# Rotary embedding's exchange of rows: products on the matrix engine, or transfers from SBUF to SBUF

## The reference

```
def apply_rope(x, cos, sin):
    xf = x.astype(jnp.float32)
    half = x.shape[-1] // 2
    x1, x2 = xf[..., :half], xf[..., half:]
    return jnp.concatenate([x1 * cos - x2 * sin, x2 * cos + x1 * sin], axis=-1)
...
proj = h @ w_in[l]
q_m, k_m, v_m, q_d, k_d, v_d, gate_m, gate_d = jnp.split(proj, IN_SPLITS, axis=-1)
qm, km = apply_rope(q_m), apply_rope(k_m)      # 8 heads of 64
qd, kd = apply_rope(q_d), apply_rope(k_d)      # 16 half-heads of 64
```

## Time and profile before

| | us |
|---|---|
| median of 3 runs | 1110.25 |
| lowest and highest | 1108.62, 1110.39 |
| profiled execution, from its first to its last instruction (span) | 1101.0 |

### The profile page before, as it was taken

How to read it: one execution, slowest core, us unless ns; L and a number is a source line. 1 busy time by engine, 2 the same in 40 slices (tenths; PEclk the granted TensorE clock), 3 DMA queues, 4 the chain that set the end, 5 groups by cost and what they waited for, 6 DMA issues and landing times.

```text
span 1101.0 us, 19063 instructions
## 1 busy us (share of the span) xinstructions
PE 917.8 (83%) x8322; PEld 709.9 (64%) x8322; DVE 540.7 (49%) x1004; ACT 347.3 (32%) x678; POOL 61.8 (6%) x81
## 2 busy tenths in 40 slices
PE   5998999999999998999999998666667565667665
PEld 5786787479999887988899975333434333334332
DVE  4446677857888856887866743121211111211121
ACT  3421155236767634545553341010100000000001
POOL 3102710000000000000010000000000000000000
PEclk9899999989999999999999999888878888988889
DMA  9442474474553565654449689999999999999994
GB/s 332 132 161 106 150 276 154 154 229 154 189 194 114 222 223 213 214 202 160 147 159 359 269 323 425 427 424 428 428 429 424 428 427 427 425 429 427 427 428 198
DMA packets 79034, 314.68 MB, mean 286 GB/s; under 512 B 3471, under 2 KB 27312, under 8 KB 62432
## 3 DMA queue, kind: packets, MB, share of 16 engines
q1 hardware_dynamic: 75204, 302.30, 69.7%
q0 software_dynamic: 3600, 11.04, 3.3%
q10 hardware_dynamic: 140, 0.04, 0.0%
HBM read 312.31 MB, written 1.06 MB: 285 GB/s over the span
## 4 chain that ended last, share of the span: by engine, by line
PE 61%; DMA 27%; DVE 6%; ACT 3%; issue 2%; SPq 0%; ACTq 0%; DVEq 0%
PE ps L468 59%; DMA w<-in_w_up 21%; DMA w<-in_w_gate 3%; DMA w<-in_w_down 2%; DMA w<-in_w_in 1%; DVE sp L1794 1%; PE ps L2593 0%; PE ps L553 0%; PE ps L2044 0%; ACT sp L1785 0%; ACT hts L2688 0%; ACT pr L1065 0%; PE ps L978 0%; ACT ht L1833 0%; DVE gm L2239 0%
## 5 line engine op out<-in xcount | busy, mean ns | idle before, releaser
L468 PE MATMUL ps<-w,xg 128*32 128x256 f32 x2048 | 156.4, 473 | 110.8 <-DMA w<-in_w_up 87.4
L468 PE MATMUL ps<-hb,sp 128*128 128x256 f32 x1824 | 229.8, 286 | 0.0
L468 PEld LDWEIGHTS ps<-hb,sp 128*128 128x128 f32 x1824 | 221.4, 190 | 6.9 <-issue 6.2
L468 PEld LDWEIGHTS ps<-w,xg 128*32 128x32 f32 x2048 | 88.2, 135 | 178.2 <-issue 157.2
L1794 DVE TENSOR_TENSOR sp<-w,sp 128x1024 fp32r<-128x1024 f32 x122 | 144.7, 1219 | 42.7 <-ACT sp L1785 42.6
L1785 ACT ACTIVATE sp<-w 128x1024 fp32r<-128x1024 f32 x122 | 122.1, 1050 | 47.7 <-PE ps L468 47.7
L2752 DVE TENSOR_TENSOR cst<-ps,cst 64x256 f32<-64x256 f32 x32 | 13.7, 428 | 227.9 <-ACT cst L2684 227.9
L2684 ACT ACTIVATE cst<-ps 64x256 f32<-64x256 f32 x32 | 12.1, 377 | 328.6 <-PE ps L468 328.6
L2767 DVE TENSOR_TENSOR ost<-ps,cst 32x256 f32<-32x256 f32 x120 | 50.4, 420 | 100.1 <-PE ps L468 97.3
L468 PE MATMUL ps<-w,hts 128*32 128x256 f32 x1024 | 62.1, 382 | 14.8 <-ACT hts L2688 11.1
L468 PE MATMUL ps<-ht,w 128*128 128x256 f32 x256 | 61.6, 400 | 2.3 <-DMA w<-in_w_in 2.2
(11 more groups left out here) (399 smaller groups left out, 1141.4 us busy)
## 6 DMA issues: line engine op xcount, KB each, us to landing
w<-in_w_down SPq DMA_DIRECT2D x36, 2048.0 KB, 36.3
w<-in_w_gate SPq DMA_DIRECT2D x32, 2048.0 KB, 28.3
w<-in_w_up SPq DMA_DIRECT2D x32, 2048.0 KB, 32.3
w<-in_w_in SPq DMA_DIRECT2D x14, 2048.0 KB, 8.8
w<-in_w_up SPq DMA_DIRECT2D x22, 1024.0 KB, 7.6
w<-in_w_ada SPq DMA_DIRECT2D x8, 2048.0 KB, 9.4
w<-in_w_out SPq DMA_DIRECT2D x4, 2048.0 KB, 8.6
w<-in_w_ada POOLq DMA_DIRECT2D x8, 768.0 KB, 4.9
```

The costliest lines, as they stand in the source:

```text
L468: return q.eng.matmul(o, l, r, start=start, stop=stop, skip_group_check=True)
```

## The change

The constant matrix `perm` goes. Its signs move into the table of sines, whose first 32 rows of each head are now negative. Instead of the product, ACT issues four transfers from SBUF to SBUF right after it has evicted a half: each copies 32 partitions of 512 numbers (64 KB) to the place of their partner, in one of two tiles, `rot0` and `rot1` in turn. Before them ACT waits for its own eviction, and from the third rotation on for the rotation two before, which read the same tile. DVE waits for the four transfers and multiplies the tile with the sines in place; the other two instructions stay.

DVE's rotation of half h moves from piece 4(h+1)+2 to piece 4(h+2)+1. The units of the first attention move from pieces 28, 31, 34, 37, 40, 43, 46, 49 to 30, 32, 35, 38, 41, 43, 46, 49; those of the second stay (52, 54, 57, 59, 62, 64, 67, 69). PSUM bank 5 is unused in this stage. A semaphore in the second pass over the experts is replaced by another.

```
@@ const_layout, const_table
-    names = [("ident", 128), ("ones", 128), ("perm", 128), ("cos", 256), ("sin", 256),
+    names = [("ident", 128), ("ones", 128), ("cos", 256), ("sin", 256),
...
-    put("perm", pm)
...
-    put("sin", np.sin(ang).astype(np.float32).T[p % 32])
+    put("sin", np.sin(ang).astype(np.float32).T[p % 32] * np.where(p % 64 < 32, -1.0, 1.0)[:, None])
@@ block_kernel
-        rt = sb("rt", 42144, 512)
+        rot = [sb("rot0", 42144, 512), sb("rot1", 49312, 512)]
...
-        A_AT = [28 + 3 * u if u < 8 else 52 + 5 * (u - 8) // 2 for u in range(NU)]
+        A_AT = [30 + 11 * u // 4 if u < 8 else 52 + 5 * (u - 8) // 2 for u in range(NU)]
...
+        def rotate_sc(q, h):
+            r, src = ROPES.index(h), q_half(h)
+            q.wait_ge(s["q_ev"], h + 1)
+            if r > 1:
+                q.wait_ge(s["rope"], 3 * r - 3)
+            for o, i in ((0, 32), (32, 0), (64, 96), (96, 64)):
+                q.eng.dma_start(rot[r % 2][o:o + 32, :], src[i:i + 32, :]).then_inc(s[f"rot{r % 2}"], 16)
@@ proj2_pe
-                if part == 1 and h - 1 in ROPES:
-                    r = ROPES.index(h - 1)
-                    q.wait_ge(s["q_ev"], h)
-                    mm(q, take(q, 5), C["perm"], q_half(h - 1)).then_inc(s["rope_mm"], 1)
-                    free[5] = [(s["rope"], 3 * r + 1)]
@@ proj2_sc, behind the eviction
+                    if h in ROPES:
+                        rotate_sc(q, h)
@@ proj2_ve
-                if g % 4 == 2 and g // 4 - 1 in ROPES:
-                    h = g // 4 - 1
+                if g % 4 == 1 and g // 4 - 2 in ROPES:
+                    h = g // 4 - 2
                     r = ROPES.index(h)
-                    qv = v(q_half(h), 2)
-                    q.wait_ge(s["rope_mm"], r + 1)
-                    q.wait_ge(s["rope"], 3 * r)
-                    e.tensor_tensor(rtv, v(psum[5], 2), sinb, MUL).then_inc(s["rope"], 1)
+                    qv, rtv = v(q_half(h), 2), rotv[r % 2]
+                    q.wait_ge(s[f"rot{r % 2}"], 64 * (r // 2 + 1))
+                    e.tensor_tensor(rtv, rtv, sinb, MUL).then_inc(s["rope"], 1)
                     e.tensor_tensor(qv, qv, cosb, MUL).then_inc(s["rope"], 1)
                     q.wait_ge(s["rope"], 3 * r + 2)
                     e.tensor_tensor(qv, qv, rtv, ADD).then_inc(s["rope"], 1)
@@ moe_ve, second pass
-                e.tensor_scalar(rk, rk, -float(NSLOT), None, ADD).then_inc(s["m_rk"], 1)
-                q.wait_ge(s["m_rk"], 1)
+                e.tensor_scalar(rk, rk, -float(NSLOT), None, ADD).then_inc(s["m_y"], 1)
+                q.wait_ge(s["m_y"], 5)
```

More of the change, by code:

```diff
@@ L105 @@
         "r_ya", "r_yv", "r_n", "wo_mm", "x1",
-        "hi", "split", "half_mm", "u_z", "u_ev", "u_c", "u_v", "u_s", "a_hi", "a_lo", "dn_mm", "x_ffn", "q_ev", "rope_mm", "rope",
+        "hi", "split", "half_mm", "u_z", "u_ev", "u_c", "u_v", "u_s", "a_hi", "a_lo", "dn_mm", "x_ffn", "q_ev", "rot0", "rot1", "rope",
         "od_sq", "mg_mm", "mg_v", "mg_hi", "mg_lo", "od_mm", "od_n", "od_hi", "od_lo", "o2_mm", "x_mix",
@@ L110 @@
         *["m_" + n for n in ("P", "g_mm", "xg_v", "xg_a", "pw_v", "pw_t", "pw", "gu", "sg", "hh", "tr", "ht",
-                                                "dn", "os", "cb", "y")], "m_rk", "f_a", "f_v"]
+                                                "dn", "os", "cb", "y")], "f_a", "f_v"]
 class Count:
@@ L1970, in block_kernel @@
         Qv = [v(t, 4) for t in Q]
-        rtv = v(rt, 2)
+        rotv = [v(r, 2) for r in rot]
         UNITS2 = [(f, pr, blk) for f in ("moba", "diff") for pr in range(4) for blk in range(2)]
         NU = len(UNITS2)
-        A_AT = [28 + 3 * u if u < 8 else 52 + 5 * (u - 8) // 2 for u in range(NU)]
+        A_AT = [30 + 11 * u // 4 if u < 8 else 52 + 5 * (u - 8) // 2 for u in range(NU)]
         ROPES = (2, 3, 4, 5, 6, 7, 8, 9)
```

## The result

| | us |
|---|---|
| before, median of 7 runs | 1110.12 (1108.13 to 1110.51) |
| changed, median of 7 runs | 1113.58 (1110.33 to 1118.05) |
| ratio | 1.0048, 95% interval 1.0031 to 1.0065 |
| profiled execution of the changed kernel: its time, its span | 1112.72, 1110.9 |

The change makes the kernel slower by 0.48%, 5.3 us by the ratio (3.4 to 7.2 by its interval; the two medians lie 3.5 us apart). The forecast was 1110.8 and no change; the measured time lies 0.08 us above the stated range. A few executions of either kernel ran in a slower state with a lower granted clock, and the ratios leave them out.

The account below looks back on a forecast made before the run. PE was taken to bound the projection stage, DVE close behind. Products saved 3.64 us against 4.2 us of PE waits: +0.55 on span 1101.0, and 9.25 to the median gave 1110.8 us, range 1107.6 to 1113.5 (8 in 10).

Parts of the forecast that it names:

- What bounds the stage: Second block's projections with attention: PE sets the stage, busy 63.21 of 63.38 us; shifts there pass whole to the end.
- The heart: Piece 45: unit 4's probability copy comes behind unit 5's exponentials and the weight copies; PE waits about 3 us.
- DVE and ACT as the chain: From piece 30 on, DVE and ACT hand work to each other in fixed order, so PE alone no longer sets the stage.
- the worked schedule: DVE's and ACT's order followed from half 5's eviction (469.82 us) to unit 5's transposes at 518.1 us.
- The size of a transfer's time: SBUF to SBUF transfers of a half, 4 x 64 KB: landing taken as under 5 us.
- The price of an issue: ACT after each of eight evictions: four DMA issues at 0.36 us each; eviction to next instruction 2.1 us.
- rival B: ACT's issues cost 0.59 us each, holding three evictions on the hand-over 0.9 us longer: +2.7, 1113.5 us; chance 0.14.
- The clock: PE's granted clock behind the wait at piece 45: the sum had no term for a slower clock.
- The saving: Eight permutation products taken off PE in the projection stage, 0.455 us each: 3.64 us.
- The wait for a transfer: DVE's rotations in the projection stage: never wait for the transfers, costed at nothing.
- A: PE stays the projection stage's bound, so 3.64 us come through: 1106.6 us; chance 0.22 with partial gains over 2.2 us.
- C: Transfers land 8 us after issue behind weight loads, delaying half 5's rotation on DVE: +2.4, 1113.2 us; chance 0.06.

Follow-up runs that it names:

- e6: The kernel before with only unit 4 of the first attention moved from piece 40 to 41; ratio 1.0051, stage 144.72 us.
- e2: The changed kernel with all transfers issued by GpSimd's queue between its own loads, none by ACT; ratio 1.0018, stage 143.54 us.
- e16: The changed kernel, its own unit places, with ACT's transfer issues behind the two weight copies of the same piece; ratio 0.9986, stage 140.18 us.
- e4: The changed kernel with the first attention's units three pieces apart from 31, the second's two pieces later; ratio 0.9995, stage 140.15 us.
- e11: The changed kernel with units three pieces apart (31 to 52, second attention from 54) and ACT's issues behind the weight copies; ratio 0.9964, stage 135.30 us.
- e1: The kernel before with only the first attention's units at the changed kernel's places, products kept; ratio 1.0060, stage 146.25 us.
- e3: The changed kernel with two of each half's four transfers issued by ACT and two by GpSimd; ratio 1.0012, stage 142.83 us.
- e5: The changed kernel with unit 4 of the first attention back at piece 40; ratio 1.0024, stage 141.16 us.
- e7: The changed kernel with transfers issued by GpSimd and units three pieces apart (from 31, second attention from 54); ratio 0.9975, stage 137.57 us.

## Why the prediction was wrong

Right, and shown by the traces:
- What bounds the stage, and that what happens in it goes to the end whole: the stage's +5.3 us is the ratio's +5.3.
- The heart: unit 4's copy falls behind unit 5's exponentials and the weight copies, PE waits about 3 us. Measured 3.2 in both profiles of the changed kernel, and made by that one place alone in e6.
- DVE and ACT as the chain. Shifted by the 2.8 us with which the changed profile starts, the worked schedule has the rotation of half 5 end at 482.2, measured 482.6; the maximum of unit 0 at 485.4, measured 485.8. From there each eviction with issues adds what the issues were priced too low, and little else is off.
- The size of a transfer's time: 5.0 us to landing in the median, the edge of the "under 5" that was taken, and up to 7.2. The 3 us that the prediction drew from the Trainium skill (page "DMA: Bandwidth & Descriptors", section "Queues, rings and completion order", the engines' turns between queues) was too short.

Wrong:
- **The price of an issue**, the step "I take 0.36 each". 0.61 was measured, and the hold from eviction to the next ACT instruction is 3.1 us, not 2.1. By unit 2's exponentials the schedule is 2.2 us late, at unit 3's issues 3.2, and so it stays: the probability copy of unit 4 ends at 522.20 (521.83 + 0.37), worked out 516.2 + 2.8 = 519.0. This is rival B in its place and its size: it had 0.59 an issue and three of them on the hand-over, +2.7. That its 1113.5 meets the median of 1113.58 is luck beyond that: against the kernel before it said +3.3, the ratio and the stage say +5.3, and the 2 us in between are the clock (below, 1.4) and 0.5 us more lateness than it had. I gave it 0.14 on the ground that only one issue at the start was that long; those were issues of a few rows or a small block from HBM, not of 32 rows of SBUF, and the row did not bear on it. The figure of the Trainium skill that the prediction set beside it (page "DMA: Bandwidth & Descriptors", section "Anatomy of one DMA", about 50 ns of dispatch) is further off as a price for the engine: the row of the profile, which holds the whole issue and not the dispatch alone, is 0.61 us on ACT, and 0.50 on GpSimd, the path for which it is told.
- **The clock**, a term that the sum did not have. A wait of 3.2 us is followed by 1.2 GHz: unit 5's transposes come 77.11 us after the first row of projection products with PE's full rate (448.42), and 71.93 before (445.62); of these 5.2 us 0.55 were forecast, 3.2 are the copy's lateness against the schedule, and about 1.4 are the clock. The prediction put nothing for it and gave no reason; the one wait of this kind in the trace before, of 1.44 us, had no such tail.
- **The saving**, 8 x 0.455 = 3.64, read as the distance from the product's start to the next product's start. It left out what the product takes from the rows behind it: 48 projection products take 6.10 us after a product and 5.69 without. True price 0.86, together 6.9. The error changed nothing in the forecast of the time, since PE only waited for ACT and DVE there, but it hid how much there was to win. It shows in the waits: up to unit 5's transposes the forecast had 4.2 us of them and 10.6 came, 3.2 more by this saving and 3.2 more by the issues.
- **The wait for a transfer**, costed at nothing. "DVE never waits for the transfers" did not hold: it waited 2.9 us for those of half 2, and from 463.87 to the end of unit 0's maximum at 485.83 it had no gap. ACT's weight copy of 474.63 would have let it start the split behind it at about 475.7 in place of 476.18, so I estimate that at most 0.5 us of this wait reaches the attention.

The sum as it came out: products -6.9, waits +10.4 (12.0 against 1.6), clock +1.5, together +5.0, measured +5.3.

Of the rivals, A was the ceiling only, and the argument against it ("the old trace waits in the very spacing") held. C's sign was seen, but its 2.4 us were not: 0.5 at most in the changed kernel, by the estimate above. Where the first transfers were issued later it counts for more: DVE's wait for them was 7.0 us in e2 and 5.8 in e16, and PE's for half 5's rotation 2.81 and 1.60 against 1.43.

What I had not seen is that two costs of nearly 5 us each stand against a saving of 6.9. With one of them alone the new kernel comes out even (e16 and e4, +0.5 us of stage each), with both it loses 5.3, with neither (e11) it gains 4.4. In the kernel before, where nothing is saved, the places alone cost 5.0 us (e6) to 6.6 (e1, where the clock stayed down for longer). That e2, e3 and e16 gain different amounts at the uneven places is explained by their traces only in part: e2's extra wait for half 5 is seen, the rest is within the intervals.

## What to carry to other kernels

Here a DMA issued by a compute engine cost that engine its issue time when something useful stood behind it, and little when the datapath still had work: put the issues after work that the datapath can still be doing, not between a wait and that work. Where engines meet at semaphores in written order, moving a unit by one step can put a short instruction behind a long block that waits for another engine; before moving it, list what stands ahead of each of its short steps at its new place. And price a product by the whole period with and without it, since the gap to the next start leaves out what it does to the stream behind it.

## What the runs showed of the hardware

- An SBUF to SBUF transfer of 32 partitions by 2 KB: issue 0.61 us on ACT, 0.50 us on GpSimd, landing after 2.0 to 7.2 us, median 5.0, beside a weight stream (the changed kernel; issued by GpSimd in e2, 1.8 to 7.4, median 5.2).
- ACT's sequencer issues DMAs while its datapath works on earlier instructions: in e16 four issues beside two 1 us copies left 0.46 us idle.
- Waits of PE of 2.65 us and more (e16, e2, e3, the changed kernel, e1, e6) were each followed by 1.2 GHz, a granted clock of 0.50, for 3 to 4 us; in e1 and behind e2's wait of 2.81 for 6 to 7 us, and no run shows why. Behind single waits of 1.4 us it stayed at 1.00. Between them both happened: 2.2 us in e5, in e7 and at 492.92 in the changed kernel without, 2.14 us in e3 and 1.77 in e4 with about 3 us at 0.50.
- One fp32 product of 128 x 128 with 512 columns amid fp32r products costs PE 0.86 us a time, of which 0.45 show from its start to the next row's (half to half 5.69, 6.55 and 7.41 to 7.48 us with none, one and two).
